# Layers' beginnings in another order, and block attention with its probabilities scaled on ScalarE

## The reference

```python
h = rms_norm(x, norm_mix[l])
(q_m, k_m, v_m, u_s, ..., gate_a, gate_b, gate_c) = split_columns(h @ w_in[l])
q_m = apply_rope(...); k_m = apply_rope(...)
y_a = moba_attention(q_m, k_m, v_m) @ w_up_moba[l]       # 8 heads x 64, softmax(q k / 8) v
y_s = gelu(s5_ssm(u_s, ...))                             # diagonal state space, 32 groups x 16
glu_a, glu_b = split(y_s @ ssm_w_glu[l], 2)
y_b = glu_a * sigmoid(glu_b)
merged = sigmoid(gate_a) * y_a + sigmoid(gate_b) * y_b + sigmoid(gate_c) * y_c
x = x + merged @ w_out[l]
```

## Time and profile before

| | us |
|---|---|
| three runs | 1770.32, 1771.11, 1775.61 |
| median | 1771.11 |
| the profiled execution, its own time | 1776.62 |
| its span, from the first to the last instruction | 1774.9 |
| PE busy in the span | 1702.5 (96%) |
| DVE, ACT, POOL busy | 1405.5, 1055.4, 158.1 |
| mean granted TensorE clock | 0.993 |

### The profile page before, as it was taken

One profiled execution on the slowest core, in us unless ns is written; L12 is line 12 of the kernel. 1 busy time (PEld: TensorE's weight loads), 2 busy tenths in 40 slices (PEclk: granted clock), 3 DMA queues, 4 the chain that ended last, 5 costly groups with the idle time before them and its releaser, 6 DMA issues. The chain is left out here.

```text
span 1774.9 us, 23666 instructions
## 1 busy us (share of the span) xinstructions
PE 1702.5 (96%) x9485; PEld 1379.8 (78%) x9485; DVE 1405.5 (79%) x1761; ACT 1055.4 (59%) x1220; POOL 158.1 (9%) x218
## 2 busy tenths in 40 slices
PE   7999989999999999998999999999999999999996
PEld 5687767788888788775778788888888888888885
DVE  5698578766555589857967699989898989899996
ACT  4234655465344523555646577777777777787765
POOL 7240002000000325000200100000000000000010
PEclk9999999999999999999999999999999999999999
DMA  8344522457552534543124699999999999999993
GB/s 263 116 143 170 190 95 85 147 184 238 177 179 95 181 121 143 180 171 115 60 94 155 224 396 379 394 374 394 370 392 388 374 390 376 389 377 390 363 396 135
DMA packets 219156, 434.93 MB, mean 245 GB/s; under 512 B 19164, under 2 KB 61800, under 8 KB 219048
## 3 DMA queue, kind: packets, MB, share of 16 engines
q1 hardware_dynamic: 212664, 419.45, 65.4%
q0 software_dynamic: 3520, 11.76, 1.7%
q10 hardware_dynamic: 2864, 2.23, 0.4%
HBM read 422.93 MB, written 10.49 MB: 244 GB/s over the span
## 5 line engine op out<-in xcount | busy, mean ns | idle before, releaser
L1648 DVE TENSOR_TENSOR split_e<-ring,split_e 128x2048 fp32r<-128x2048 f32 x264 | 598.4, 2288 | 40.3 <-ACT split_e L1063 39.9
L1063 ACT ACTIVATE split_e<-ring 128x2048 fp32r<-128x2048 f32 x264 | 503.1, 1919 | 149.3 <-PE bank L3142 124.6
L3140 PE MATMUL bank<-split_e,fx_e 128*128 128x512 f32 x704 | 278.6, 396 | 0.4 <-DVE fx_e L2430 0.4
L3142 PE MATMUL bank<-split_e,fx_e 128*128 128x512 f32 x704 | 274.7, 390 | 0.0
L3141 PE MATMUL bank<-split_e,fx_e 128*128 128x512 f32 x704 | 274.3, 390 | 0.0
L3142 PEld LDWEIGHTS bank<-split_e,fx_e 128*128 128x128 f32 x704 | 132.1, 188 | 28.1
L3140 PEld LDWEIGHTS bank<-split_e,fx_e 128*128 128x128 f32 x704 | 132.2, 188 | 26.6 <-DVE fx_e L2430 0.6
L3141 PEld LDWEIGHTS bank<-split_e,fx_e 128*128 128x128 f32 x704 | 132.4, 188 | 26.2
L3140 PE MATMUL bank<-split_e,f_actT_e 128*128 128x512 f32 x352 | 137.6, 391 | 1.1 <-DVE f_actT_e L2438 1.1
L3142 PE MATMUL bank<-split_e,f_actT_e 128*128 128x512 f32 x352 | 137.0, 389 | 0.0
L3141 PE MATMUL bank<-split_e,f_actT_e 128*128 128x512 f32 x352 | 137.0, 389 | 0.0
(11 more groups left out here) (639 smaller groups left out, 3308.0 us busy)
## 6 DMA issues: line engine op xcount, KB each, us to landing
ring<-in_moe_w_gate SPq DMA_DIRECT2D x40, 2048.0 KB, 13.8
ring<-in_moe_w_up SPq DMA_DIRECT2D x40, 2048.0 KB, 13.8
ring<-in_moe_w_down SPq DMA_DIRECT2D x40, 2048.0 KB, 13.6
ring<-in_w_in SPq DMA_DIRECT2D x28, 2048.0 KB, 7.9
ring<-in_ffn_w_gate SPq DMA_DIRECT2D x11, 1024.0 KB, 5.4
ring<-in_ffn_w_up SPq DMA_DIRECT2D x11, 1024.0 KB, 7.9
ring<-in_ffn_w_down SPq DMA_DIRECT2D x11, 1024.0 KB, 8.7
ring<-in_ssm_w_glu SPq DMA_DIRECT2D x8, 1024.0 KB, 6.2
```

The lines of the kernel that those rows point to most:

```text
L1063: nc.scalar.activation(split_e[j % NBUF][:, HI, :], ring[:, s * PIECE + i * HGRP:s * PIECE + (i + 1) * HGRP], ACT.Copy).then_inc(split_hi, 1)
L1648: V.tensor_tensor(split_e[j % NBUF][:, LO, :], ring[:, s * PIECE + i * HGRP:s * PIECE + (i + 1) * HGRP], split_e[j % NBUF][:, HI, :].bitca ...
L3140: mm(bank, a[HI], w[HI], start=first, stop=False)
L3142: return mm(bank, a[LO], w[HI], start=False, stop=last_one)
```

## The change

It has four parts.

1. **Layer 0's beginning.** On PE x's transposes come before both transposes of parameters; the second pair goes into U_U behind column group m = 0, the row factors behind m = 2 (in both layers). ACT sums the squares of x before it copies the first parameters, and takes 1/rms right behind the evacuation of x's transposes. DVE makes the diagonals first, and copies the row factors and multiplies the first half of `uT` before it computes the constants, the second half behind them. The constants' temporaries move from `s5c` to `gates`, because `s5c` now holds the row factors meanwhile.
2. **Layer 1's beginning.** DVE's work is laced: a half of `e_lo`, one weight rest, row factors, half of `uT`, one rest, the other half of `e_lo`, two rests, the other half of `uT`.
3. **Block attention.** DVE keeps only the reciprocal (`moba_sum`, which increments `ms_neg`); the two scalings become ACT activations of kind Copy with a scale per row, in step s behind `moba_pT(s - 1)` and the weight splits. The list `MS_TURNS` gives the count of `ms_neg` at each turn.
4. **Gated unit.** `y` is written with a quarter in place of a half, tanh needs no scale, and the last multiplication by 0.5 goes.

```diff
@@ ScalarE, start @@
+            act.wait_ge(x_in, 16)
+            for t in range(NT):
+                squares(x[:, :, :], t, h_tok, ss)
             act.wait_ge(par_ps, 1)
             nc.scalar.activation(params[:, 0:P], B[0][:, 0:P], ACT.Copy).then_inc(par_ready, 1)
             act.wait_ge(par_ready, 1)
             evac_norm(0, hT[:, :, :], gain_mix, 0, hT_ready)
...
+            act.wait_ge(consts, 2)
+            sum_squares(x[:, :, :], 0, tiles=())
+            halve_rstd(0)
             act.wait_ge(par_ps, 2)
...
@@ ScalarE, block attention @@
+                def moba_norm(h):
+                    p, o = mp_[h % 2], 2 * (h % 2)
+                    act.wait_ge(ms_neg, ms_neg_at(l, "sum", h))
+                    nc.scalar.activation(p[:, 0:P], p[:, 0:P], ACT.Copy, scale=rs[:, o:o + 1])
+                    nc.scalar.activation(p[:, P:3 * P], p[:, P:3 * P], ACT.Copy, scale=rs[:, o + 1:o + 2]).then_inc(ms_norm, 1)
...
-                    nc.scalar.activation(glu_t[i % 2], B[1][:, :], ACT.Tanh, scale=0.5).then_inc(glu_th, 1)
+                    nc.scalar.activation(glu_t[i % 2], B[1][:, :], ACT.Tanh).then_inc(glu_th, 1)
...
                     if s < 2:
                         unit_split_hi(l, U_GLU + 1, [2 + s])
+                    if s < MH:
+                        moba_norm(s)
@@ VectorE @@
+            row_factors(0)
+            state_input(0, 0)
             dve.wait_ge(sin_ready, 1)
...
+            state_input(0, 1)
             dve.wait_ge(sin_ready, 2)
...
-                link(V.tensor_scalar(y_hi, yflat, 0.5, None, ALU.mult))
-                V.scalar_tensor_tensor(y_lo, yflat, 0.5, y_hi.bitcast(F32), ALU.mult, ALU.subtract).then_inc(y_ready, 1)
+                link(V.tensor_scalar(y_hi, yflat, 0.25, None, ALU.mult))
+                V.scalar_tensor_tensor(y_lo, yflat, 0.25, y_hi.bitcast(F32), ALU.mult, ALU.subtract).then_inc(y_ready, 1)
...
-                    link(V.reciprocal(rs[:, o:o + 2], rs[:, o:o + 2]))
-                    V.tensor_scalar(p[:, 0:P], p[:, 0:P], rs[:, o:o + 1], None, ALU.mult)
-                    V.tensor_scalar(p[:, P:3 * P], p[:, P:3 * P], rs[:, o + 1:o + 2], None, ALU.mult).then_inc(ms_norm, 1)
+                    V.reciprocal(rs[:, o:o + 2], rs[:, o:o + 2]).then_inc(ms_neg, 1)
...
-                    link(V.scalar_tensor_tensor(gl_tmp[t], g, 1.0, glu_y[t], ALU.add, ALU.mult))
-                    link(V.tensor_scalar(merged[:, t, n_ * 512:(n_ + 1) * 512], gl_tmp[t], 0.5, None, ALU.mult))
+                    link(V.scalar_tensor_tensor(merged[:, t, n_ * 512:(n_ + 1) * 512], g, 1.0, glu_y[t], ALU.add, ALU.mult))
@@ TensorE @@
                     if m % 2 == 1:
                         last.then_inc(ready, 1)
+                    between(m)
...
+                def between(m):
+                    if m == 0 and l == 0:
+                        transpose_parameters()
+                    if m == 2:
+                        row_factors(l)
```

More of the change, by code:

```diff
@@ L1649, in piece_lo @@
                                 split_e[j % NBUF][:, HI, :].bitcast(F32), ALU.subtract).then_inc(split_lo, 1)
-            c_ = [s5c[:, i, :] for i in range(14)]
+            c_ = [s5t[:, i - 4, :] if 4 <= i < 12 else s5c[:, i, :] for i in range(14)]
             def rstd_diagonals(l):
@@ L1705, in _, with early_lo @@
             for l in range(DEPTH):
-                if l > 0:
-                    rstd_diagonals(l)
-                for half in range(2) if l > 0 else ():
+                def early_lo(half):
                     dve.wait_ge(x_hi, xs_base(l) + X_E + half + 1)
@@ L2550, in _ @@
             pe.wait_ge(consts, 1)
-            pe.wait_ge(rows_set, 16 * 6)
-            tr(B[0][:, 0:P], rows[:, 0, :], ident[:, :]).then_inc(par_ps, 1)
             pe.wait_ge(x_in, 16)
@@ L2579, in features_out @@
                     for k in range(KD):
-                        if norms is not None and m == 0 and k % 2 == 0:
+                        if m == 0 and k % 2 == 0:
                             pe.wait_ge(hT_ready, norms + k // 2 + 1)
@@ L2623, in _ @@
                 last.then_inc(ab_ps, 1)
-                for t in range(NT):
-                    pe.wait_ge(diag_ready, NT * l + t + 1)
-                    last = mm(B[3][:, t * P:(t + 1) * P], ones[:, :], rstd_diag[:, t, :], start=True, stop=True)
-                last.then_inc(row_rstd_ps, 1)
                 def ab_sums():
```

87 lines of the change are left out of this document (53 added, 34 removed).

## The result

The changed kernel took 1780.51 us (median of 8 runs, 1778.22 to 1785.87) against 1773.97 us of the kernel before in 8 runs (1769.86 to 1775.94): a ratio of 1.0041, 95% interval 1.0028 to 1.0053. It is slower by 5 to 9 us. The forecast was 1772.1, no change that can be told; the range ended at 1776.0. The forecast stood on the median of the first three runs of the kernel before, 1771.11; the median of all eight lies 2.9 us higher, and that part of the distance to 1780.51 does not come from the change.

What follows compares the result with a forecast made beforehand. TensorE was taken to be late only where it waits, so each edit was priced by its waits and clock effects: -3.8 + 0.3 + 2.4 + 1.05 + 1.0 = +0.95, giving 1772.1 us; range 1766.5 to 1776.0.

Steps and rivals of the forecast that it cites:

- block attention: Moving the two scalings from VectorE to ScalarE changes TensorE's waits: +1.05 us in layer 0, +1.0 in layer 1.
- layer 0's beginning: Fill(2) starts 5.5 us earlier, less 1.7 for the clock's slow level in U_U: together -3.8 us (-4.4 to -3.4).
- first transposes: Block attention's first head: scalings stand behind the weight's high part and end at 221.7, +0.70 us.
- first two merges: Block attention: small shifts at the first two merges, +0.18 us, leaving TensorE 0.88 late.
- weight rest: Block attention at 239.96: TensorE's wait for VectorE's weight rest shrinks as VectorE sheds work, -0.55 us.
- third merge: Block attention: ScalarE's copies stand ahead of exponentials and tanh, for whose merge the gated unit waits, +0.60 us.
- head 7 and behind: End of block attention: the last merges get shorter, -0.12 us.
- Layer 1's beginning: The wait moves from fill(0) to fill(2), 5.6 us; split pairs cost +0.3, a slow clock stretch +2.4.
- Relief for VectorE: Rival: VectorE's earlier finish takes back each block attention's +0.88; each layer comes to -0.5, total 1769.0 us; chance 0.10.
- transposes do not count: Rival: in layer 0 transposes don't count for TensorE's clock, which rises as early as before; 1770.4 us; chance 0.15.
- GpSimd in VectorE's way: Rival: GpSimd's work slows VectorE in layer 0, fill(2) waits until 50, a slow stretch follows; 1778.1 us; chance 0.09.
- The change doesn't do what it says: Rival: layer 0's uT is ready no earlier, row factors waiting for something else on TensorE; about 1778 us; chance 0.03.

Runs made afterwards that it cites:

- fold alone: The kernel before with only the fourth part, the half taken into y: 1771.36 us against 1773.86, ratio 0.9986.
- first experiment: The changed kernel with block attention's scalings back on VectorE, beginnings and gated unit still changed: 1775.34 us against 1774.03 of the kernel before, ratio 1.0012.
- early fills: The kernel before with GpSimd's four fills pulled ahead of its masks: 1773.01 us against 1775.72, ratio 0.9988.
- exact products: The first experiment's kernel plus unread products, 9 and 12 in the beginning, 11 ahead of layer 1's fill(2): 1774.70 us against 1775.32 of the kernel before, ratio 0.9998.

## Why the prediction was wrong, point by point

The medians moved by 6.5 us where the sum had +0.95. Two of its terms carry this miss, about equally: block attention (+2.05, measured 5 to 6.6) and layer 0's beginning (-3.8, measured 0.1, between -1.6 and +2.0).

**Block attention, +1.05 and +1.0: the first step that failed.** Measured were 5 to 6.6 us (1.0041 against 1.0012, and 1.0037 alone). TensorE's waits, before and after in layer 0, against the forecast's terms:

| wait of TensorE | before | after | change | forecast |
|---|---|---|---|---|
| first transposes | 0.62 | 1.31 | +0.69 | +0.70 |
| first two merges | 1.08, 1.08 | 1.17, 1.44 | +0.45 | +0.18 |
| weight rest | 1.39 | 0.96 | -0.43 | -0.55 |
| head 5 | 0.97 | 1.25 | +0.28 | +0.24 |
| third merge | 1.20 | 1.80 | +0.60 | +0.60 |
| head 7 and behind | 0.64 | 0.81 | +0.17 | -0.12 |

The mechanism stands, place by place, and the waits came to +1.8 in place of +1.05 (in layer 1 to +1.4 in place of +1.0). Mis-sized were the merges, where ScalarE's tanh follows late, and the end. But the step that failed is another: the sum priced waits alone. With them came a slow stretch in each of the eight block attentions of the four profiles that have the scalings on ScalarE and no unread products. Of the 18 in the nine other profiles without unread products there, six had one. At 1.6 us each this is two thirds of 3.2, 2.1 us more; with the waits 5.3 us. The clock was watched at waits of 3 us and over; here several waits of 0.8 to 1.8 us stood within 35 us, and the level fell as TensorE came back from 1.25 and 1.80 us of waiting. That products which nobody reads hold the level (0 of 6 block attentions, in three kernels) and that the ratio falls with them shows the cause; the size of what they give back is less certain (3.4 us by the ratios, 1.9 in the profiles).

Block attention from its first scores to the end of its last output product, in both layers:

| kernel | block attention, us | with a slow stretch |
|---|---|---|
| before, profile shown | 41.8, 42.1 | none |
| before, two more | 41.9, 42.1 and 41.9, 43.7 | one of four |
| fold alone | 41.4, 41.6 | none |
| first experiment | 41.4, 43.2 | one of two |
| changed kernel | 45.2, 45.1 | both |
| scalings alone | 46.6, 45.4 | both |
| changed, products in the waits | 44.2, 44.2 | none |

**Layer 0's beginning, -3.8: wrong, though the profile agreed.** In the profile shown fill(2) moved from 52.4 to 48.91, as worked out (47.1 and 1.7 for the clock, 48.8). Every step of it held: U_U at 13.36, the level rising near 18.3, fill(0) without a wait. The step that failed is its base: the profiled execution was taken for the kernel. From U_U's start to fill(2) five profiles of the old beginning give 39.0, 37.9, 38.0, 34.1 and 33.6 us. In the first three VectorE's operation took 3.33 us beside GpSimd's fills, and a slow stretch followed in fill(0); in the last two neither came. Six profiles of the new beginning without products there give 34.7 to 35.8. So the new order takes away the price of a stall that comes in some executions, and is 0.5 us or more worse in the others. (U_U itself starts at 12.4 to 13.4 in the new order and at 12.7 to 13.4 in the old one. Counted from the start of the profile fill(2) stands at 47.1 to 48.9 in the new order, at 51.3 to 52.4 in the old one with the stall and at 46.3 and 47.3 without it.) The stall is not gone from the new order either. In one of the six, the changed kernel with products in block attention's waits, it took

```profile
24.19 3.07 DVE L1648 TENSOR_SCALAR cosr<-cosr 128x64 f32<-128x64 f32 x1
```

and cost little, since VectorE waits there for the row factors, which TensorE had at 26.8. The fills moved early take the stall away in the old order, and the mean falls by 2.3 us. The prediction had seen the 3.33 us and taken 3.1 of it off the new side only. How often the stall comes is open. With the means of these positions (47.8 for the new order, 51.6 and 46.8 for the old one) the beginning alone would gain nothing if one old execution in five had the stall; the 2.3 us of the early fills fit about one in two, and then a gain of about 1 us, which the interval of the beginning alone (0.9991 to 1.0011) still allows. Both shares are estimates.

**Layer 1's beginning, +0.3 and +2.4: right in kind, too large.** The wait moved to fill(2) (5.36, forecast 5.6), the level fell at 632.7 and rose at 639.6, 4.0 us behind the restart, just under the range's short end. The lead went from -0.3 to +1.5 where it was to be 2.7. The end of VectorE's work moved by -0.3 and not +0.3.

**The rivals.** Relief for VectorE does count, but for the fold alone: 0.43 us at one wait. Transposes can raise the level: in the first experiment's profile it rose at 9.1 while TensorE had done nothing but x's transposes, whose rows go from

```profile
L2566 PE MATMUL bank<-ident,x x11: 421/421/447, 5.9 to 8.1; 128*128 128x128 f32 x11
...
L2566 PE MATMUL bank<-ident,x x3: 273/361/421, 8.7 to 9.1; 128*128 128x128 f32 x3
```

(durations, min/median/max ns). In two more profiles of the new beginning it rose at 10.2 and 10.7, ahead of U_U too; in the other three of the six, the changed kernel's among them, the same transposes did not do it, and it rose inside U_U at 15.4 to 18.3. The rule of the Trainium skill, "TensorE: Matmul & The Clock Gate", Part 4, that transposes do not count, is not what this chip did here, and the measurement decides. GpSimd in VectorE's way was there: in the kernel before, and in the versions with unread products in the beginning, whose earlier VectorE ran into the fills (1.45 and 1.38 us). "The change doesn't do what it says" did not come: `uT` was ready, and fill(0) did not wait.

**The chances.** 0.13 was given to slower by over 0.3%, nearly all of it for two cases in layer 0's beginning (0.09 and 0.03), the rest for the forecast's tail. None of the cases was a slow stretch in block attention, since the one profile had none there.

## What to carry to other kernels

A wait's price is not its length alone: where the change adds to several waits of about 1 us close together, TensorE's clock can fall among them, and the profile of the kernel before needs not show it, since whether it does varies from one execution to the next. Before a sum is made against one profiled execution, ask of each long operation in it whether its like elsewhere took as long; a stall of 3 us in a 0.2 us operation can belong to the execution and not to the kernel; two more profiles showed here that it doesn't come each time, and are too few to tell how often. It is also a matter of place: work that a change brings forward can run into it, as the products' 1.6 us in layer 0 did, of which 0.3 were left. Work moved from one engine to another that TensorE waits for in turn is priced by the receiver's order: on ScalarE the two scalings delayed the tanh behind them, and putting them first only moved the delay.

## What the runs showed of the hardware

- A small VectorE copy, or operation with a constant, of 0.17 to 0.19 us by itself, that began while GpSimd was filling tiles or 0.1 us ahead of it was held in most cases. It then ended with the last fill: 3.33 us (23.97 to 27.3) in the profile of before, 1.19 us (26.17 to 27.36) in a second profile, 1.45 us (25.85 to 27.3) in the exact products' one. It is not a rule: in the third profile of the kernel before a copy was let go between two fills (0.35 us, 25.66 to 26.01), and in the changed kernel an operation that began 0.1 us ahead of the first fill was not held at all (23.98, 0.20 us) and one beside the fills for 0.2 us only (24.73, 0.39 us). Operations of two sources (0.19 us each) and a reciprocal (0.35, as elsewhere) went on beside the fills from 24.0 to 26.2. Beside GpSimd's arithmetic it was otherwise: in the early fills' profile an operation of two sources of 0.19 us took 0.98 (25.32 to 26.30) while GpSimd added two tiles (25.24 to 26.26). The Trainium skill, "GPSIMD Engine Reference", Key points, says that the two engines share their interfaces to SBUF, and that VectorE's instructions contend that are in a two-port mode or have two inputs in SBUF. The first kind may be what is held beside the fills; the second was not held there, and was beside the arithmetic. No run here separates the kinds further.
- Nine unread products of the unit matrix from 1.85 us on brought the level up by 6.5 us in one profile and by 5.3 in another, about when x landed; the profiles of the new beginning without them have it at 9.1 to 18.3. It was worth 1.6 us of U_U. By fill(2) 0.3 were left, since VectorE, though earlier, was held beside GpSimd's fills.
